# Memory keys and values of an encoder block: token-major product with k outermost and whole weight rows

## The chip, the cores and the metric

The kernel is one launch on one core of a Trainium2 chip. The metric is device time in microseconds (us), from the core's start to its end. The engines are named as the profile names them: PE (TensorE, matrix products), PEld (its loads of stationary operands), DVE (VectorE), ACT (ScalarE), POOL (GpSimd) and SP (SyncE, which here issues nearly all DMAs).

## The reference

One layer of a hybrid encoder block, 512 tokens by 1024 channels in fp32. Only the cross-attention branch to 256 memory tokens is shown in full, since the change lies there:

```python
h = rms_norm(x, norm_mix_pre[l])
z = h @ w_in[l]                    # qa, ka, va, qx, pin and the gates
oa = window_attention(qa, ka, va, rel_bias, sinks)   # 16 heads, 2 key groups, chunks of 64
mkv = rms_norm(mem, norm_mem[l]) @ w_mem_kv[l]       # (256, 1024) @ (1024, 1024)
mk, mv = jnp.split(mkv, 2, axis=-1)                  # keys and values, 4 heads of 128
ox = memory_attention(qx, mk, mv)
op = multiscale_pool(pin, w_pool_map[l], pool_scale[l])
merged = gates[0] * (oa @ w_branch_a) + gates[1] * (ox @ w_branch_x) + gates[2] * (op @ w_branch_p)
x = x + rms_norm(merged @ w_out[l], norm_mix_post[l])
# then a SwiGLU FFN with d_ff = 2816 between two RMS norms
```

## The kernel before, in words

Every fp32 product is made of three float32r products: an operand is split into a high part (`w_hi`, a rounding copy on ACT, line 403) and a low part (`w_lo`, the difference, on DVE, line 408), and hi·hi, hi·lo and lo·hi are summed in PSUM (`three`, line 1337). So every weight tile costs ACT and DVE a pass before PE can use it.

Work is laid out by `plan()` as 66 steps. A step is mostly one tile: 128 output channels over the whole contraction of 1024 (8 slices `k` of 128). Steps 0 to 7 are the memory projection (`mem` 4 to 7, the values, then `mem` 0 to 3, the keys), then `k`, `v`, eight `q`, four `qx`, four `pin`, gates and merges. Each engine has its own program, written by hand, which goes through the steps with a loop `for s in range(NS)`. In step s, ACT and DVE split the weights of step s + 2 into one of three slots `w_hi[s % 3]`, `w_lo[s % 3]`, which needs the product of step s - 1 to be over. Raw weights come in chunks of two steps (two loads of 512 KB) into `raw[0]`, `raw[1]` and, once, `raw_early`; SP issues all loads in the order of its program and waits on `weights_split` before it overwrites a buffer.

The memory projection is feature-major. A tile has weight columns as stationary operand and the 256 memory tokens as moving one: 24 products of 256 columns. ACT evicts the tile to `mvT` or `mk` (`take`, line 717). The first two tiles are made in two halves of the contraction (`first_tiles`), so that they can begin when half the tokens and half of a chunk have arrived. Before them PE runs 40 transposes of an identity matrix (`warm_up`, line 1472).

The norm of the memory tokens is applied after the product. Their sums of squares are made in step 9 (`mem_sum`), POOL raises them to the power -1/2, and then the scale takes two ways. For the keys, which have the tokens along the free axis, DVE builds two diagonal matrices (`mem_diagonal`, line 1075), PE spreads them over all partitions by a product with ones (`mem_scale`, line 1372, in step 11) and DVE multiplies `mk` (line 1058). For the values, PE transposes `mvT` after step 12 (line 1500) and DVE scales on the way out of PSUM (line 1153). In the same stretch the norm of x (loaded by SP only after the last split of the transposed x, on `turned_split`) becomes a row `x_row` (lines 1113, 1490, 1117), by which DVE scales `k`, `v` and `q` as it evicts them (lines 934 and 956).

The tiles of the first steps take PSUM banks 0 to 3 in turn; a tile waits until the tile before it in its bank is evicted. Attention units begin in step 15 (scores, bias, softmax, turn, output; one unit in two steps). In `maxima` DVE waits for the scores, for unit 0 first reverses the bias table (line 975), then adds the bias (line 978, two instructions), and for the first chunk pair overwrites the masked half with -1e30 (line 984).

## Time and profile before

| | |
|---|---|
| median of 3 runs | 802.42 us (802.08 to 802.8) |
| profiled execution, its own time | 802.09 us |
| its span in the trace | 800.3 us |
| PE busy | 788.7 us (99% of the span) |
| DVE busy | 481.0 us (60%) |
| ACT busy | 332.4 us (42%) |
| mean granted clock of TensorE | 0.998 |

The span is what the trace covers; the rest of the execution's time (1.79 us) lies around it. Products on PE are pipelined and their ends are modelled, so the distance between the starts of two products tells more than the length of one. Idle time of an engine costs something only where the engine is the one that is waited for.

### The profile page before, as it was taken

The numbers are of one execution on the slowest core, as the hardware profiler recorded it, in microseconds if no ns is written. First come the engines' busy times: TensorE is split into PE (matmuls) and PEld (weight loads), VectorE is DVE, ScalarE is ACT, GpSimd is POOL, SyncE is SP. The second block draws the span as 40 slices with busy tenths as digits, with TensorE's granted clock in tenths as the row PEclk, the third lists the DMA queues.
The fourth block names the chain that finished last, engine by engine and source line by source line (L and its number), as shares of the span: only waits on it lengthen the run. The fifth ranks groups of instructions, "written<-read, shape, count | busy, mean of one in ns | idle before, by whom it ended". The sixth has DMA issues, their size and how long they took to land.

```text
span 800.3 us, 11623 instructions
## 1 busy us (share of the span) xinstructions
PE 788.7 (99%) x4624; PEld 688.0 (86%) x4624; DVE 481.0 (60%) x597; ACT 332.4 (42%) x558; POOL 47.1 (6%) x99
## 2 busy tenths in 40 slices
PE   8999999999999999999999999999999999999997
PEld 7978778777778888888888999999999999888885
DVE  5755657666434633625655589888888887733222
ACT  5731544454335223223443455444444446632111
POOL 0020000444000000000001210000000000000000
PEclk9999999999999999999999999999999999999999
DMA  8961221312212333333371003333333344641011
GB/s 289 304 185 52 84 75 53 106 54 71 87 53 61 99 105 106 106 105 134 130 263 52 26 30 108 105 104 105 105 105 105 105 131 157 218 151 52 1 53 52
DMA packets 68502, 85.76 MB, mean 107 GB/s; under 512 B 3552, under 2 KB 61424, under 8 KB 68464
## 3 DMA queue, kind: packets, MB, share of 16 engines
q1 hardware_dynamic: 68288, 85.23, 32.5%
q8 instruction: 26, 0.43, 0.2%
q14 instruction: 12, 0.10, 0.0%
q10 hardware_dynamic: 176, 0.01, 0.0%
HBM read 83.12 MB, written 2.11 MB: 106 GB/s over the span
## 4 chain that ended last, share of the span: by engine, by line
PE 91%; DVE 4%; DMA 1%; issue 1%; ACT 1%; POOL 1%; SPq 0%; DVEq 0%; POOLq 0%; ACTq 0%
PE pair L1337 84%; PE pair L1446 1%; DMA raw<-in_w_mem_kv 1%; PE pair L1427 1%; PE pair L1460 1%; PE pair L1435 1%; PE pair L1465 1%; POOL B_f L657 1%; DVE T_f L1224 1%; DVE op_lo L1204 1%; DVE T_lo L1231 0%; PE pair L1361 0%; ACT probs L694 0%; DVE k_dup L934 0%; PE pair L1344 0%
## 5 line engine op out<-in xcount | busy, mean ns | idle before, releaser
L408 DVE TENSOR_TENSOR w_lo<-raw,w_hi 128x1024 fp32r<-128x1024 f32 x66 | 84.1, 1277 | 95.4 <-ACT w_hi L403 95.4
L1337 PE MATMUL pair<-hT_hi,w_hi 128*128 128x512 f32 x336 | 135.6, 403 | 0.0
L1337 PE MATMUL pair<-hT_hi,w_lo 128*128 128x512 f32 x336 | 131.2, 390 | 0.0
L1337 PE MATMUL pair<-hT_lo,w_hi 128*128 128x512 f32 x336 | 130.9, 390 | 0.0
L403 ACT ACTIVATE w_hi<-raw 128x1024 fp32r<-128x1024 f32 x66 | 69.5, 1055 | 105.8 <-PE pair L1337 90.1
L1337 PE MATMUL pair<-T_hi,op_hi 128*128 128x256 f32 x320 | 90.6, 283 | 0.5 <-DVE op_lo L1204 0.5
L1337 PE MATMUL pair<-T_lo,op_hi 128*128 128x256 f32 x320 | 90.6, 283 | 0.0
L1337 PE MATMUL pair<-T_hi,op_lo 128*128 128x256 f32 x320 | 90.5, 283 | 0.0
L1337 PEld LDWEIGHTS pair<-hT_hi,w_hi 128*128 128x128 f32 x336 | 63.1, 188 | 14.2 <-issue 1.0
L1337 PEld LDWEIGHTS pair<-hT_lo,w_hi 128*128 128x128 f32 x336 | 63.2, 188 | 13.4 <-issue 1.0
L1337 PEld LDWEIGHTS pair<-hT_hi,w_lo 128*128 128x128 f32 x336 | 63.0, 188 | 13.5
L1337 PE MATMUL pair<-wd_hi,df_hi 128*128 128x512 f32 x176 | 68.5, 389 | 0.0
L1337 PE MATMUL pair<-wd_lo,df_hi 128*128 128x512 f32 x176 | 68.5, 389 | 0.0
L1337 PE MATMUL pair<-wd_hi,df_lo 128*128 128x512 f32 x176 | 68.5, 389 | 0.0
L1337 PE MATMUL pair<-B_hi,op_hi 128*128 128x256 f32 x240 | 67.9, 283 | 0.0
L1337 PE MATMUL pair<-B_lo,op_hi 128*128 128x256 f32 x240 | 67.9, 283 | 0.0
L1337 PE MATMUL pair<-B_hi,op_lo 128*128 128x256 f32 x240 | 67.9, 283 | 0.0
L1337 PEld LDWEIGHTS pair<-T_hi,op_hi 128*128 128x128 f32 x320 | 61.4, 192 | 0.7 <-DVE op_lo L1204 0.7
L1337 PEld LDWEIGHTS pair<-T_hi,op_lo 128*128 128x128 f32 x320 | 61.4, 192 | 0.0
L1337 PEld LDWEIGHTS pair<-T_lo,op_hi 128*128 128x128 f32 x320 | 61.4, 192 | 0.0
L408 DVE TENSOR_TENSOR wd_lo<-raw,wd_hi 128x1024 fp32r<-128x1024 f32 x22 | 26.9, 1222 | 35.6 <-ACT wd_hi L403 35.6
L1337 PEld LDWEIGHTS pair<-B_hi,op_hi 128*128 128x128 f32 x240 | 46.1, 192 | 0.0
(194 smaller groups left out, 1549.5 us busy)
## 6 DMA issues: line engine op xcount, KB each, us to landing
raw<-in_w_in SPq DMA_DIRECT2D x42, 512.0 KB, 4.8
raw<-in_w_ffn_up SPq DMA_DIRECT2D x22, 512.0 KB, 4.7
raw<-in_w_ffn_gate SPq DMA_DIRECT2D x22, 512.0 KB, 4.2
raw<-in_w_ffn_down SPq DMA_DIRECT2D x22, 512.0 KB, 4.0
raw<-in_w_branch_a SPq DMA_DIRECT2D x8, 512.0 KB, 4.1
raw<-in_w_out SPq DMA_DIRECT2D x8, 512.0 KB, 3.6
raw<-in_w_mem_kv SPq DMA_DIRECT2D x6, 512.0 KB, 7.1
xT_in<-in_x_t SPq DMA_DIRECT2D x4, 512.0 KB, 8.8
```

What stands on the lines that cost most here:

```text
L403: eng.activation(split_at(s)[0], raw_view(s), ACT.Copy).then_inc(weights_hi, 1)
L408: eng.tensor_tensor(lo, raw_view(s), hi.bitcast(F32), ALU.subtract).then_inc(weights_split, 1)
L657: pool.tensor_tensor(plain[b][:, :, P * (t % 2):P * (t % 2) + P], h2_at(t, h, True).bitcast(F32), h2_at(t, h, False).bitcast(F32), ALU.add ...
L1204: dve.tensor_tensor(lo[:, :, :], op_source(m), hi[:, :, :].bitcast(F32), ALU.subtract).then_inc(ops_split, 1)
L1224: dve.tensor_tensor(plain[t][:, :, :], plain[a][:, :, :], plain[b][:, :, :], ALU.subtract)\
L1337: ins = pe.matmul(dst, a, b, start=first and n == 0, stop=last and n == 2, skip_group_check=onto)
L1427: ins = pe.matmul(scores[:, pr // 2, at:at + KEYS], q[lo:lo + 64, 2 * a + pr % 2, ch, :, :].rearrange("p j t -> p (j t)"), k_dup[lo:lo + 6 ...
L1435: ins = pe.matmul(scores[:, i // 2, at:at + N_MEM], qx[:, a, P * i:P * i + P], mk[:, a, :], start=True, stop=True)
L1446: ins = pe.transpose(turned[:, at // 4, P * (at % 4):P * (at % 4) + P], probs[:, i, :], ident[:, :])
L1460: ins = pe.matmul(bk(O_BANK)[64 * half:64 * half + 64, 2 * P * c:2 * P * c + 2 * P], v_c[:, 2 * b + c, 64 * a:64 * a + 64], probs[:, i:i + ...
L1465: ins = pe.matmul(bk(O_BANK), mv[:, m, a, :], probs[:, 4 * m:4 * m + 4, :], start=(m == 0), stop=(m == MT - 1))
```

## The change

The memory projection becomes token-major: the tokens are the stationary operand (128 tokens) and 512 weight columns the moving one. `k` is the outermost loop, and one step is one slice `k`: a whole weight row block of 128 x 1024 is loaded (4 KB in a row in memory, where before it was 1 KB), split, and multiplied into four PSUM banks that are open through all eight steps (banks 0 and 1 keys and values of tokens 0 to 127, banks 2 and 3 those of tokens 128 to 255). `k`, `v` and `mem_sum` get banks of their own (4, 5, 7). The transposed memory tokens come in four loads of 256 KB instead of two of 512 KB, and the first weight row in two halves of 256 KB; the loads of the transposed x move between them.

After the last row ACT evicts the four banks (`mem_take`), keys to `mk_rows` and values straight to `mv`. In step 10 DVE scales both by the token's norm, now one number per partition (4 instructions). After step 12 PE transposes `mk_rows` in place of `mvT`, and DVE copies the result to `mk`. `mem_diagonal` and `mem_scale` are gone.

DVE's instructions for `x_diag` move from step 10 to step 9, and the splits of x to steps 2, 4, 6 and 7. In `maxima`, the reversal of the bias and the masked half come ahead of the wait for the scores, and the first half of the masked units is added in two smaller instructions. POOL waits for the maxima of unit 4 before it begins the pooling branch.

```diff
-X_HI = {1: (0,), 3: (1,), 4: (2,), 5: (3,)}
-X_LO = {2: (0,), 4: (1,), 5: (2, 3)}
+X_SPLITS = {2: 0, 4: 1, 6: 2, 7: 3}
-    steps = [[("mem", h)] for h in (4, 5, 6, 7, 0, 1, 2, 3)]
+    steps = [[("mem", k)] for k in range(KT)]
-    steps[MEM_SUM + 2].append(("mem_scale", 0))
-        O_BANK, SUM_BANK = 3, 7
+        O_BANK, OUTER_BANK = 3, {"k": 4, "v": 5, "mem_sum": 7}
+        def mem_bank(m, h):
+            return bk(2 * m + h)
+            def load_row(k):
+                if k == 6:
+                    sp.wait_ge(weights_split, 4)
+                load_half(k // 2, k % 2, row_in[k])
+            load_mem(0)
+            load_half(0, 0, half_in, slice(0, 512))
+            load_half(0, 0, row_in[0], slice(512, 1024))
+            load_mem(1)
+            load_row(1)
+            load_row(2)
+            load_mem(2)
+            load_row(3)
+            load_mem(3)
+            load_row(4)
             load_x(0)
+            load_row(5)
+            load_row(6)
             load_x(1)
+            load_row(7)
+            load_chunk(4)
             load_x(2)
             load_x(3)
+            def mem_take(m, h):
+                act.wait_ge(tile_full, KT)
+                dst = mv[:, m, :, :] if h else as4(mk_rows[:, m, :])
+                act.activation(dst, as4(mem_bank(m, h)), ACT.Copy).then_inc(mem_rows_out, 1)
             def mem_evicted(t):
                ...
+                dve.wait_ge(mem_rows_out, 2 * MT)
+                for m in range(MT):
+                    dve.wait_ge(mem_rstd_ready, m + 1)
+                    for rows in (as4(mk_rows[:, m, :]), mv[:, m, :, :]):
+                        dve.tensor_scalar(rows, rows, rstd[:, c + m:c + m + 1], None, ALU.mult).then_inc(mem_scaled, 1)
-                if s == X_SCALE:
+                if s == X_SQUARES:
                     for t in range(TT):
                         dve.wait_ge(rstd_ready, NORM_X + t + 1)
             def maxima(u):
                 kind, a, b = unit_of(u)
+                if u == 0:
+                    dve.wait_ge(bias_loaded, 16 * 16)
+                    ...
+                    link(dve.tensor_copy(bias[:, :, :, :].rearrange("p g a k -> p (g a) k"), back))
+                    dve.wait_ge(smalls_loaded, 16 * 4)
+                if kind == "a" and b == 0:
+                    if u >= 1:
+                        dve.wait_ge(o_full, u)
+                    dve.memset(probs[:, 0:4, 0:CHUNK], -1e30).then_inc(masked, 1)
                 dve.wait_ge(scores_full, u + 1)
-            first_tiles()
-            for s in range(2, NS):
+            for k in range(KT):
+                mem_row(k)
+            for s in range(KT, NS):
+            def mem_row(k):
+                def part(m, h):
+                    cols = slice(4 * h, 4 * h + 4)
+                    whi, wlo = (w[k % 3][:, cols, :].rearrange("p a c -> p (a c)") for w in (w_hi, w_lo))
+                    return three(mem_bank(m, h), whi, wlo, memT_hi[:, k, P * m:P * m + P], memT_lo[:, k, P * m:P * m + P],
+                                 k == 0, k == KT - 1, swap=True)
+                pe.wait_ge(mem_split, k + 1)
+                ...
+                    pe.wait_ge(weights_split, k + 1)
+                    for m in range(MT):
+                        for h in range(2):
+                            ins = part(m, h)
```

Two places show how the instructions move. The first is PE at the start of the projection. In these rows `w_hi_51`, `w_hi_52` and `w_hi_53` are the three weight slots, `w_lo_55` the low part of the first, and `pair` is PSUM. Before:

```order
L1472 MATMUL pair<-ident 128x128 x39
L1337 MATMUL pair<-memT_hi,w_hi_51 128x256 [waits mem_split,half_split,ones_ready]
L1337 MATMUL pair<-memT_lo,w_hi_51 128x256
L1337 MATMUL pair<-memT_hi,w_lo_55 128x256
L1337 MATMUL pair<-memT_hi,w_hi_51 128x256 [waits mem_split]
...
L1337 MATMUL pair<-memT_hi,w_hi_52 128x256 [waits half_split]
...
L1337 MATMUL pair<-memT_hi,w_hi_51 128x256 [waits mem_split,weights_split]
```

After:

```order
L1517 MATMUL pair<-ident 128x128 x39
L1379 MATMUL pair<-w_hi_51,memT_hi 128x512 [waits half_split,mem_split,ones_ready]
L1379 MATMUL pair<-w_lo_55,memT_hi 128x512
L1379 MATMUL pair<-w_hi_51,memT_lo 128x512
L1379 MATMUL pair<-w_hi_51,memT_hi 128x512
...
L1379 MATMUL pair<-w_hi_51,memT_hi 128x512 [waits weights_split]
...
L1379 MATMUL pair<-w_hi_52,memT_hi 128x512 [waits weights_split,mem_split]
...
L1379 MATMUL pair<-w_hi_53,memT_hi 128x512 [waits weights_split,mem_split]
```

The products of the first row need one load of tokens and one half row. A row's twelve products are 512 columns wide, and from the second row on each row has one wait for its weights and its tokens.

The second place is DVE from the diagonals of x to the eviction of the projected `v`, steps 9 to 11. Before:

```order
L1113 TENSOR_SCALAR x_diag<-ident,rstd 128x128 [waits rstd_ready] x4
L1054 TENSOR_SCALAR meansq<-pair 128x2 [waits tile_full]
L408 TENSOR_TENSOR w_lo_56<-raw_49,w_hi_52 128x1024 [waits weights_hi]
L1117 COPY x_row<-pair 128x512 [waits x_scaled]
L934 TENSOR_TENSOR k_dup<-pair,x_row 64x512 [waits tile_copied,pads_ready,tile_full,x_row_ready]
L934 TENSOR_TENSOR k_dup<-pair,x_row 64x512 x3
L956 TENSOR_TENSOR vT<-pair,x_row 128x512 [waits tile_full]
L956 TENSOR_TENSOR q<-pair,x_row 128x8x64 [waits tile_full]
L1075 TENSOR_SCALAR diag<-ident,rstd 128x128 [waits mem_rstd_ready] x2
L408 TENSOR_TENSOR w_lo_57<-raw_50,w_hi_53 128x1024 [waits weights_hi]
L956 TENSOR_TENSOR q<-pair,x_row 128x8x64 [waits tile_full]
L1058 TENSOR_TENSOR mk<-mk,pair 128x1024 [waits tile_copied,tile_full]
```

After:

```order
L1158 TENSOR_SCALAR x_diag<-ident,rstd 128x128 [waits rstd_ready] x4
L415 TENSOR_TENSOR w_lo_55<-raw_49,w_hi_51 128x1024 [waits weights_hi]
L1100 TENSOR_SCALAR meansq<-pair 128x2 [waits tile_full]
L1105 TENSOR_SCALAR mk_rows<-mk_rows,rstd 128x512 [waits mem_rstd_ready,mem_rows_out]
L1105 TENSOR_SCALAR mv<-mv,rstd 128x512
L1105 TENSOR_SCALAR mk_rows<-mk_rows,rstd 128x512 [waits mem_rstd_ready]
L1105 TENSOR_SCALAR mv<-mv,rstd 128x512
L415 TENSOR_TENSOR w_lo_56<-raw_49,w_hi_52 128x1024 [waits weights_hi]
L1162 COPY x_row<-pair 128x512 [waits x_scaled]
L969 TENSOR_TENSOR k_dup<-pair,x_row 64x512 [waits pads_ready,tile_full,x_row_ready]
L969 TENSOR_TENSOR k_dup<-pair,x_row 64x512 x3
L991 TENSOR_TENSOR vT<-pair,x_row 128x512 [waits tile_full]
```

The diagonals of x stand ahead of a weight split that they followed. The four scalings of keys and values stand ahead of the split of step 13 and of the evictions of `k` and `v`; the diagonals of the memory norm and the scaling of `mk` are gone.

## Rows read from the trace of the kernel before

**Rows 1.** page, part 1, and waits of the whole run (engine line waited for: us, times, longest)
```profile
PE 788.7 (99%) x4624; PEld 688.0 (86%) x4624; DVE 481.0 (60%) x597; ACT 332.4 (42%) x558; POOL 47.1 (6%) x99
...
PE pair L1372 <- DVE diag L1075: 1.3, 1, 1.3
...
PE pair L1337 <- DVE w_lo L408: 0.5, 1, 0.5
PE pair L1337 <- DVE op_lo L1204: 0.5, 1, 0.5
```

**Rows 2.** windows (stretch, busy per engine, PEclk, DMA share, GB/s)
```profile
2.00:29.00 27.00, 25.20 (x198) 24.79 (x199) 17.48 (x53) 18.75 (x33) 0.24 (x2) 1.00 0.96 311
```

**Rows 3.** timeline of PE (start, duration, line, operation [idle before <- releaser])
```profile
2.05 6.04 PE L1472 MATMUL pair<-ident 128*128 128x128 f32 x40 [2.05 <-POOL ident L597]
9.33 0.36 PE L1337 MATMUL pair<-memT_hi,w_hi 128*128 128x256 f32 x1 [1.24 <-issue]
...
15.04 0.28 PE L1337 MATMUL pair<-memT_hi,w_lo 128*128 128x256 f32 x1
15.82 0.38 PE L1337 MATMUL pair<-memT_hi,w_hi 128*128 128x256 f32 x1 [0.51 <-DVE w_lo L408]
...
33.19 0.40 PE L1337 MATMUL pair<-hT_hi,w_hi 128*128 128x512 f32 x1
```

**Rows 4.** timelines of ACT and DVE, the first 23 us
```profile
6.28 1.71 ACT L737 ACTIVATE memT_hi<-memT_in,g_mem_c 128x256 fp32r<-128x256 f32 x4 [3.13 <-DMA memT_in<-in_mem]
7.89 1.13 ACT L742 ACTIVATE w_hi<-raw 128x512 fp32r<-128x512 f32 x2
...
19.02 1.06 ACT L403 ACTIVATE w_hi<-raw_early 128x1024 fp32r<-128x1024 f32 x1 [2.06 <-DMA raw_early<-in_w_mem_kv]
...
6.90 1.67 DVE L1082 SCALAR_TENSOR_TENSOR memT_lo<-memT_in,g_mem_c,memT_hi 128x256 fp32r<-128x256 f32 x4 [6.90 <-ACT memT_hi L737]
8.54 1.29 DVE L1089 TENSOR_TENSOR w_lo<-raw,w_hi 128x512 fp32r<-128x512 f32 x2
...
16.82 2.04 DVE L1144 COPY rel_row<-relT 16x18 f32<-16x18 f32 x29
...
20.11 1.23 DVE L408 TENSOR_TENSOR w_lo<-raw_early,w_hi 128x1024 fp32r<-128x1024 f32 x1 [1.24 <-ACT w_hi L403]
21.25 1.41 DVE L919 SCALAR_TENSOR_TENSOR hT_lo<-xT_in,g_pre_c,hT_hi 128x512 fp32r<-128x512 f32 x2
```

**Rows 5.** DMA issues up to 34 us (KB each, median us to landing)
```profile
xT_in<-in_x_t SPq DMA_DIRECT2D x4, 512.0 KB, 8.8
```

**Rows 6.** chain of waits, one tile (start, us, what)
```profile
44.60 5.62 PE pair L1337 x24
```

**Rows 7.** timeline of PE, around that wait and unit 0's turn
```profile
56.16 0.39 PE L1337 MATMUL pair<-hT_hi,w_lo 128*128 128x512 f32 x1
57.84 0.68 PE L1372 MATMUL pair<-diag,ones 128*128 128x128 f32 x4 [1.29 <-DVE diag L1075]
58.28 0.48 PE L1337 MATMUL pair<-hT_hi,w_hi 128*128 128x512 f32 x1
...
86.44 0.39 PE L1337 MATMUL pair<-hT_hi,w_lo 128*128 128x512 f32 x1
87.04 1.09 PE L1446 MATMUL pair<-ident,probs 128*128 128x128 f32 x8 [0.21 <-DVE probs L1006]
```

**Rows 8.** timelines of DVE and ACT, 31 to 92 us
```profile
66.87 1.40 DVE L1153 TENSOR_SCALAR mv<-pair,rstd 128x512 f32<-128x512 f32 x2
...
77.81 0.69 DVE L975 COPY bias<-bias_back 128x1024 f32<-128x1024 f32 x1 [3.56 <-PE pair L1427]
...
39.82 1.04 ACT L676 ACTIVATE square<-x_in 128x1024 f32<-128x1024 f32 x1
...
91.27 0.60 ACT L707 ACTIVATE oa_hi<-pair 128x512 fp32r<-128x512 f32 x1 [2.06 <-PE pair L1460]
```

**Rows 9.** chain of waits, output projection
```profile
423.65 10.93 PE pair L1337 x48
```

More of the change, by code:

```diff
@@ L129, in encoder_block @@
     UNIT0 = steps.index([("q", 5)])
-    copied_kinds = ("mem", "k", "v", "q", "qx", "pin", "gate")
+    copied_kinds = ("k", "v", "q", "qx", "pin", "gate")
     copied_no, merged_no = {}, {}
     for t in tiles:
-        d = copied_no if t[0] in copied_kinds else merged_no
-        d[t] = len(d) + 1
+        if t[0] != "mem":
+            d = copied_no if t[0] in copied_kinds else merged_no
+            d[t] = len(d) + 1
     def ap(t, offset, pattern):
@@ L275, in encoder_block @@
             last = {b: m for m, b in enumerate(bank_of)}
-            b = SUM_BANK if t[0] == "mem_sum" else min(range(free), key=lambda i: last.get(i, -1))
+            b = OUTER_BANK[t[0]] if t[0] in OUTER_BANK else min(range(free), key=lambda i: last.get(i, -1))
             bank_of.append(b)
             bank_before[n] = last.get(b)
-        last_in_o_bank = max(n for n, b in enumerate(bank_of) if b == O_BANK and n < step_end[UNIT0])
         first_in_o_bank = min(n for n, b in enumerate(bank_of) if b == O_BANK and n >= step_end[UNIT0])
+        def mem_bank(m, h):
+            return bk(2 * m + h)
         def sem(name):
@@ L285, in encoder_block @@
         raw_in = [sem(f"raw_in{i}") for i in range(2)]
-        early_in = sem("early_in")
-        mem_loaded = [sem(f"mem_loaded{i}") for i in range(2)]
+        mem_rows_out, mem_scaled = sem("mem_rows_out"), sem("mem_scaled")
+        mem_loaded = [sem(f"mem_loaded{i}") for i in range(MEM_PIECES)]
+        row_in = [sem(f"row_in{k}") for k in range(KT)]
         x_loaded = [sem(f"x_loaded{i}") for i in range(TT)]
@@ L338, in chunk_halves @@
                 if t == "mem":
-                    v, col = w_mem_v, P * i
-                elif t == "a":
+                    return [w_mem_kv[P * (i + h):P * (i + h + 1), :] for h in range(2)]
+                if t == "a":
                     v, col = wa_v, P * i
@@ L519, in _ @@
             sp.dma_start(scale_p[:, :], pool_scale).then_inc(smalls_loaded, 16)
-            for c in range(4, 6):
-                load_chunk(c)
+            load_chunk(5)
             sp.wait_ge(turned_split, KT)
@@ L634, in _ @@
                 pool.wait_ge(tile_copied, copied_no[("pin", g)])
+                if g == 0:
+                    pool.wait_ge(neg_max_ready, (steps.index([("pin", 0)]) - UNIT0) // 2 + 2)
                 if g >= 1:
@@ L1126, in _ @@
                     for t in steps[s - 1]:
-                        if t in copied_no and t[0] not in ("mem", "k", "v"):
+                        if t in copied_no and t[0] not in ("k", "v"):
                             scaled_take(t)
@@ L1368, in tile @@
                     return
-                if kind == "mem_scale":
-                    pe.wait_ge(diag_ready, MT)
-                    for m in range(MT):
-                        ins = pe.matmul(dst[:, P * m:P * m + P], ones[:, :], diag[:, m, :], start=True, stop=True)
-                    ins.then_inc(tile_full, 1)
-                    return
                 whi, wlo = w_hi[s % 3], w_lo[s % 3]
                 pe.wait_ge(weights_split, at_stream[("step", s)] + 1)
-                if kind == "mem":
-                    xhi, xlo, dst = memT_hi, memT_lo, dst[:, 0:N_MEM]
-                elif kind in ("a", "p", "x"):
+                if kind in ("a", "p", "x"):
                     xhi, xlo = {"a": (oa_hi, oa_lo), "p": (op_hi, op_lo), "x": (ox_hi, ox_lo)}[kind]
@@ L1454, in unit_out @@
                 else:
-                    pe.wait_ge(tile_copied, copied_no[tiles[last_in_o_bank]])
+                    pe.wait_ge(mem_rows_out, O_BANK + 1)
                 if kind == "a":
```

163 lines of the change are left out of this document (83 added, 80 removed).

## The prediction

> **What bounds the kernel now.** I read first the busy times and the list of what PE waited for [rows 1]. PE is busy for 99% of the span, and of its named waits inside the program only one is over a microsecond: 1.3 us for DVE's diagonals of the memory norm. The others are 0.5 us in the memory projection and 0.5 us in the FFN. So this is a PE-bound program: what counts is the distance between starts of products, the few holes between them, and when the first real product can begin. The granted clock is 1.00 in the projection [rows 2], which is the upper level, 2.4 GHz. Next I read PE's timeline at the start [rows 3]: warm-up transposes from 2.05 to 8.09, a hole, the first product at 9.33, a second hole before 15.82, and the first product of `k` at 33.19. Then the timelines of ACT and DVE, which make the operands [rows 4], and the loads [rows 5]. Last come the pace of a 512-column product in this stretch [rows 6], the two later places where PE waits [rows 7], the costs of copies and scalings [rows 8], and the pace of the output projection [rows 9], whose products have the form that the changed projection will have (weights moving, tokens stationary).
>
> Since almost nothing after unit 0 waits for an absolute time, a microsecond won before 90 us should arrive at the end as a microsecond. The loads there follow the splits, so they move with PE.
>
> **Start of the first product.** Before, ACT begins at 6.28, when the 512 KB of tokens have come, makes four token slices (1.71) and the halves of two tiles (1.13 for two), and DVE's first low part begins at 8.54 and takes 0.65 (half of 1.29) [rows 4]; PE follows at 9.33 [rows 3]. After, PE needs two token slices (0.86) and one half row (0.57), then DVE's 0.65: 2.1 us and some 0.15 of handing over, so 2.25 after the tokens land. They land at 6.28 at the latest, as the 512 KB did, and 256 KB must be earlier; halving only the transfer at 311 GB/s [rows 2] takes 0.8 us off, so 5.5. PE could begin at 7.75, but the warm-up ends at 8.09 and is now what is late. I take 8.1: **1.2 us won**. Bounds: 0.8 (tokens at 6.28, so PE at 8.5) and 1.25.
>
> **The hole inside the projection.** 15.04 to 15.82 is 0.78 where a product takes 0.12, so 0.66 is lost to waiting for the low part of the third tile [rows 3]. That wait is one for a chunk of two tiles. After, the equivalent is row 1. It lies behind 1.5 MB of loads, as the second half of the tokens did before; that half was there when ACT wanted it at 9.0 (7.89 plus 1.13, and no wait), so row 1 lands by 9.0, and at the mean rate of 311 GB/s from 2 us on by 7.1 [rows 2]. Add 1.06 on ACT and 1.23 on DVE [rows 4]: ready between 9.5 and 11.4. PE asks for it after twelve products, at 8.1 + 12 x 0.234 = 10.9. So a stall of 0 to 0.5; I take 0.2. Net **0.66 - 0.2 = 0.46 won**.
>
> **The products.** Before: 33.19 - 9.33 = 23.86, less 0.66, is 23.2 us for 192 products of 256 columns, 0.121 each. After: 96 of 512 columns. In the row just behind the projection 24 such products take 5.62 us, 0.234 each [rows 6]; in the output projection 48 take 10.93, 0.228 each [rows 9]. The nearer row was taken under full DMA load like the projection, so I use it: 96 x 0.234 = 22.5, and 0.1 for the first. **0.6 us won**; by the other row 1.3, which is the far bound. On the near side I set 0.4.
>
> **The norm's diagonal.** In step 11 the last product of `q` 1 starts at 56.16 and the first of `q` 2 at 58.28 [rows 7]: 2.12 where 0.23 is usual. The wait of 1.29 for DVE's diagonals and the products with ones both go. **1.89 won**, if DVE isn't late for something else. What is late next there are the transposes after step 12, which wait for the evicted `v` and now for the scaled keys. I follow DVE: x is loaded for its squares only after the last split of x, which stays near 31 us, so ACT can begin the squares as before at 39.82 [rows 8] at the latest; four of them, 1.04 each and a read-out, some 1.2 together, end at 44.6; POOL and the four diagonals, now ahead of a split, bring DVE to 45.7. Behind that wait stands the split of step 12, which PE wants at 54, so the earlier place costs nothing. Then split 1.23, the mean square, POOL's two powers (1.1), four scalings at the 0.70 that a 128 x 512 scaling out of PSUM takes [rows 8], split of step 13, `x_row` 0.7, four `k_dup` at 0.7 and `v` 0.7: 45.7 + 1.2 + 1.3 + 2.8 + 1.2 + 0.7 + 2.8 + 0.7 = 56.4. PE gets to the transposes at 8.1 + 0.2 + 22.6 = 30.9 for the end of the projection, then five tiles of 5.62 and 0.7 of small products: 59.7. The cover is 3.3 us, so the added 2.8 us of scaling cost nothing. The four evictions on ACT are 0.60 each [rows 8] and end by 34.5; `q` 0 wants its bank at 42.5. If the cover were gone, each microsecond of DVE would be one of PE.
>
> **Splits during the projection.** PE takes 2.8 us a row, ACT 1.06 and DVE 1.23, plus tokens and x (DVE 0.42 a token slice, 0.70 a slice of x, [rows 4]). The tightest point is row 4: from 11.4 on DVE has the splits of rows 2 and 3 (2.5), four token slices (1.7) and the `rel_row` copies (2.04 [rows 4]), 17.6, and the split ends at 18.9; PE wants it at 8.3 + 4 x 2.81 = 19.5. Covered by 0.6. The last slices of x end near 31.4; `k` wants them at 35.8.
>
> **Unit 0.** The turn of its probabilities waits 0.21 [rows 7]. DVE's reversal of the bias, 0.69 [rows 8], leaves the chain ahead of it, so the wait goes: **0.2 won**. For unit 4 the masked half was not on PE's path; the POOL wait stands behind maxima that DVE does before it evicts `pin` 0, so it releases nothing later. Both at nothing, and a few tenths either way at most.
>
> **Sum.** 1.2 + 0.46 + 0.6 + 1.89 + 0.2 = 4.35. The profiled execution took 802.09, so 797.7. The median of the runs is 802.42, 0.33 above it, so on that scale 798.1; I say 798.0. The bounds together: won at least 0.8 + 0.16 + 0.4 + 1.6 + 0 = 3.0 and at most 1.25 + 0.66 + 1.3 + 1.9 + 0.4 = 5.5, so 796.7 to 799.4.
>
> **Rivals.** *Late rows.* PE no longer works on two tiles from half a chunk but waits for each row; if the loads come slower than before, the holes come back eight times. Row 4 must have landed by 17.1 (19.5 less the two splits): that is 1 MB of tokens and 2.6 MB of weights in 15 us, 245 GB/s, against a mean of 311 in this stretch [rows 2]. At 200 GB/s it would land at 20.4 and PE would stand for 3.3 us: 801.3 us. For it: smaller first loads, and the trace has no row-wise load in this stretch. Against it: the rate, and rows four times as long in memory. The Trainium skill's page "DMA: Bandwidth & Descriptors", section "Measured (HBM→SBUF, 128 partitions, SWDGE, issued from GpSimd)", asks for batches of 1 MiB or more for 75% of peak, which speaks against pieces of 256 KB; here loads of 512 KB already run at 311 GB/s together, because several are in flight, so I give it little. The page "TensorE: Matmul & The Clock Gate", section "HAM oscillation — how this bites in real kernels", has a loop over k whose waits for loads make the array fall back to the slow clock; the trace's own holes of 1.24 and 0.51 us [rows 3] left the granted clock at 1.00 [rows 2], so it belongs to this rival only. *DVE takes the place of the removed wait.* The queue of step 10 and 11 grows past its 3.3 us of cover and PE stands before the transposes for what it won at the diagonal: 798.1 + 1.9 = 800.0. Against it is the working above; for it, that POOL's powers and ACT's evictions are waited for in a row. *Slower than before.* One mechanism: the last slices of x. SP holds row 6 back until row 3 is split, and row 7, the weights of `k` and `v` and the last two loads of x queue behind it. `k` wants the last slice at 35.8; its load must be in by 33.4. Up to it there are 8.4 MB, which came by 29 us before (311 GB/s from 2 us on). To end over 804.0 PE must lose 6 us here, so the load must end at 39.4, a mean of 225 GB/s; that is where it decides, and it would give 804 to 806. Loads of x did take 8.8 us to land in the median [rows 5], but queued, not slow. *Faster still*: products at 0.228 and no stall at row 1, 0.9 more: 797.2 or a little less.
>
> **Chances.** Forecast, with its own range of 796.9 to 799.2: 0.76. Faster still, 796.2 to 796.9: 0.06. Late rows, 799.2 to 801.5: 0.09. DVE, near 800: 0.05. Slower: 0.04. Range for 8 in 10: 796.7 to 800.2. What a measurement of this kernel can tell from no change is 0.2%, 1.6 us, so faster means under 800.8: 0.76 + 0.06 + 0.05 + half of the late rows is 0.91; within 0.05; slower 0.04.
>
> **What would show it.** The first product of the projection near 8.1, directly behind the warm-up; a hole under 0.5 us before row 1 and none before other rows; 96 products 0.228 to 0.234 apart; `k` beginning near 30.9 instead of 33.19; no wait between `q` 1 and `q` 2, none at the transposes, none at unit 0's turn; from there on every stretch as long as before. A first product later than 8.6, a granted clock under 1.00, or a wait of PE for DVE at the transposes would make it wrong.

## The result, and the profile after

The changed kernel takes 798.53 us in the median, the kernel before 802.42. The ratio is 0.9949, with a 95% interval of 0.9937 to 0.9962: 0.5% faster, clear of no change. One of the changed kernel's five executions took 2791 us, a slow run that isn't in the ratio; the other four took 798.0 to 798.5. The profiled execution took 798.53 us with a span of 796.7; before they were 802.09 and 800.3, so the two traces differ by 3.6 us, and this is what has to be found.

The page, part 1, and what PE waited for, as in [rows 1]:

```profile
PE 787.0 (99%) x4524; PEld 683.4 (86%) x4524; DVE 481.4 (60%) x599; ACT 332.6 (42%) x553; POOL 47.7 (6%) x99
...
PE pair L1379 <- DVE w_lo L415: 1.3, 1, 1.3
```

PE is as full as before. The wait for the diagonals (1.3) and the one in the projection (0.5) are gone, and a new one of 1.3 stands in the projection, for DVE's low part of a weight row. Next PE's timeline from the start to the first product of `k`; the columns are those of [rows 3]:

```profile
2.05 6.82 PE L1517 MATMUL pair<-ident 128*128 128x128 f32 x40 [2.05 <-POOL ident L620]
8.63 0.47 PE L1379 MATMUL pair<-w_hi,memT_hi 128*128 128x512 f32 x1
...
11.25 0.39 PE L1379 MATMUL pair<-w_hi,memT_lo 128*128 128x512 f32 x1
12.97 0.47 PE L1379 MATMUL pair<-w_hi,memT_hi 128*128 128x512 f32 x1 [1.33 <-DVE w_lo L415]
...
32.13 0.39 PE L1379 MATMUL pair<-hT_hi,w_hi 128*128 128x512 f32 x1
```

The first product begins at 8.63 instead of 9.33. The twelfth begins at 11.25, and the next one, row 1's first, would be due at 11.48 and begins at 12.97: 1.49 us lost, where the kernel before lost 0.66 [rows 3]. `k` begins at 32.13 instead of 33.19. There is no idle time before rows 2 to 7. The timelines of ACT and DVE say what row 1 waited for, and answer to [rows 4]:

```profile
5.59 0.91 ACT L758 ACTIVATE memT_hi<-memT_in,g_mem_c 128x256 fp32r<-128x256 f32 x2 [2.45 <-DMA memT_in<-in_mem]
...
9.24 0.91 ACT L758 ACTIVATE memT_hi<-memT_in,g_mem_c 128x256 fp32r<-128x256 f32 x2 [1.10 <-DMA memT_in<-in_mem]
10.51 1.06 ACT L410 ACTIVATE w_hi<-raw 128x1024 fp32r<-128x1024 f32 x1 [0.36 <-DMA raw<-in_w_mem_kv]
...
7.07 0.69 DVE L1131 TENSOR_TENSOR w_lo<-raw,w_hi 128x512 fp32r<-128x512 f32 x1
...
11.60 2.52 DVE L415 TENSOR_TENSOR w_lo<-raw,w_hi 128x1024 fp32r<-128x1024 f32 x2 [0.93 <-ACT w_hi L410]
```

ACT stands until row 1's load has landed at 10.50, splits it until 11.57, DVE makes its low part from 11.60 to 12.83, and PE starts at 12.97. Ahead of that, ACT had waited 1.10 us for the second piece of tokens, which landed at 9.24, and which only row 2 needs. The rates are in the windows of the same stretch, the kernel after first, the one before second (columns as in [rows 2]):

```profile
2.00:9.00 7.00, 6.95 (x42) 6.91 (x43) 2.23 (x4) 3.21 (x6) 0.24 (x2) 1.00 0.88 247
2.00:10.50 8.50, 8.45 (x48) 8.14 (x49) 2.95 (x6) 4.12 (x8) 0.24 (x2) 1.00 0.90 276
9.00:15.00 6.00, 4.67 (x21) 3.53 (x20) 4.22 (x7) 5.07 (x8) 0.00 (x0) 1.00 1.03 415
```

```profile
2.00:9.00 7.00, 6.04 (x40) 5.80 (x40) 2.10 (x5) 3.86 (x9) 0.24 (x2) 1.00 0.95 296
9.00:15.00 6.00, 5.67 (x47) 5.70 (x48) 4.07 (x9) 4.30 (x9) 0.00 (x0) 1.00 1.08 361
```

Up to 9 us the kernel after moved 1.73 MB (7 us at 247 GB/s), the kernel before 2.07 MB. From 9 to 15 it is the other way round: 415 GB/s where weights come in rows of 4 KB, 361 where they come in pieces of 1 KB. Order and mix of the loads differ too, so these numbers alone don't show that the row length does it. When row 1 had landed, 2.35 MB had moved (8.5 us at 276 GB/s), though in order of issue row 1 ends after 1.57 MB.

The chain of waits shows the rest. First after, then the rows of before that were not needed ahead of the prediction; columns are start, length, what:

```profile
43.18 0.34 PE pair L1410 x4
...
50.02 10.90 PE pair L1379 x48
60.92 0.88 PE pair L1547 x8
...
73.56 1.09 PE pair L1473 x16
...
83.73 0.87 PE pair L1491 x8
...
86.68 1.01 PE pair L1505 x8
...
403.97 15.27 PE pair L1379 x66
```

```profile
44.26 0.34 PE pair L1366 x4
...
64.00 0.87 PE pair L1500 x8
...
76.67 1.12 PE pair L1427 x16
...
90.20 1.01 PE pair L1460 x8
...
407.51 15.26 PE pair L1337 x66
```

Read as a ledger (before minus after; what each stretch added is the difference of two lines):

| event | before | after | won so far |
|---|---|---|---|
| first product | 9.33 | 8.63 | 0.70 |
| first product of `k` | 33.19 | 32.13 | 1.06 |
| `mem_sum`, after `k` and `v` | 44.26 | 43.18 | 1.08 |
| transposes after step 12 | 64.00 | 60.92 | 3.08 |
| scores of unit 0 | 76.67 | 73.56 | 3.11 |
| turn of unit 0 | 87.04 | 83.73 | 3.31 |
| output of unit 0 | 90.20 | 86.68 | 3.52 |
| output projection | 407.51 | 403.97 | 3.54 |
| span | 800.3 | 796.7 | 3.6 |

Everything is won before 90 us and kept for the other 710. The two `q` tiles between which PE used to stand for the diagonals are now one piece of 10.90. DVE's queue there, which the prediction added up, answers to [rows 8]:

```profile
47.54 1.23 DVE L415 TENSOR_TENSOR w_lo<-raw,w_hi 128x1024 fp32r<-128x1024 f32 x1 [2.45 <-ACT w_hi L410]
...
49.57 0.49 DVE L1105 TENSOR_SCALAR mk_rows<-mk_rows,rstd 128x512 f32<-128x512 f32 x1 [0.73 <-POOL rstd L648]
...
50.77 0.48 DVE L1105 TENSOR_SCALAR mv<-mv,rstd 128x512 f32<-128x512 f32 x1
...
55.84 0.69 DVE L991 TENSOR_TENSOR vT<-pair,x_row 128x512 f32<-128x512 f32 x1
```

The four scalings take 0.40 each from start to start, and `v` is evicted at 56.53, while PE wants it at 60.92: a cover of 4.4 us.

### The profile page after: what moved, and what is told of

Its sections match the earlier page's. It is cut to its first block, busy times and chain, and to the rows that moved or that the text cites. A ratio compares the mean times of both kernels' runs of the same rounds, so it can differ in the third digit from the quotient of the medians.

```text
span 796.7 us, 11430 instructions
## 1 busy us (share of the span) xinstructions
PE 787.0 (99%) x4524; PEld 683.4 (86%) x4524; DVE 481.4 (60%) x599; ACT 332.6 (42%) x553; POOL 47.7 (6%) x99
## 4 chain that ended last, share of the span: by engine, by line
PE 93%; DVE 3%; DMA 1%; issue 1%; POOL 1%; ACT 1%; SPq 0%; DVEq 0%; POOLq 0%; ACTq 0%
PE pair L1379 87%; PE pair L1491 1%; PE pair L1473 1%; PE pair L1505 1%; DMA raw<-in_w_mem_kv 1%; PE pair L1480 1%; PE pair L1510 1%; POOL B_f L682 1%; DVE T_f L1266 1%; DVE op_lo L1246 1%; DVE T_lo L1273 0%; PE pair L1405 0%; PE pair L1386 0%; DVE sum_odd L1261 0%; DVE f L1278 0%
```

## The experiments

Each kernel was timed beside the kernel before, in three groups: experiments 1 to 4, 5 to 8 and 9 to 11. "Ratio" is to the kernel before in the same group, with its 95% interval. The kernel before took 802.31, 802.24 and 802.00 us in them, so medians of different groups can differ by 0.3 us without any change. One thousandth is 0.8 us. The later stretch repeats closely: from `mem_sum` to the output projection, a stretch that only experiment 5 changes, the two traces of the changed kernel and those of its other eight variants below agree within 0.05 us (360.78 to 360.83).

**1. The diagonal alone.** In the kernel before, `mem_diagonal` goes ahead of `x_row` and the evictions of `k`, `v` and `q`, and nothing else changes:

```diff
                 if s == X_SCALE + 1:
+                    mem_diagonal()
                     dve.wait_ge(x_scaled, 1)
-                if s == MEM_SUM + 2:
-                    mem_diagonal()
```

> The kernel before, with DVE's two diagonals of the memory norm moved ahead of the copy of x_row and the evictions of k, v and q 0 in step 11. The products with ones stay. If the 1.97 us between q 1 and q 2 were a wait of 1.3 for DVE's queue plus 0.7 of products, the wait goes and the span falls by 1.3 us (802.1 to 800.8), PE going straight from q 1 to the products with ones. Rival: the wait is set by the norm itself (POOL's powers, at 49 us) or by the eviction of k, whose bank q 2 or the scale takes; then PE still waits there, less than 0.4 us is won.

Measured: 801.27 us, ratio 0.9987 (0.9978 to 0.9997). Its chain of waits:

```profile
56.46 0.59 PE pair L1371 x4
...
57.06 5.74 PE pair L1336 x24
```

The diagonal product no longer waits. The first product of `q` 2 begins 0.99 us behind the last of `q` 1, where it was 2.12 [rows 7] and is 0.23 in the changed kernel. So 1.13 of the 1.89 us there, six tenths, could be had by moving one call: the wait was one of order on DVE, not of a late result from POOL. The rest, 0.76, is the products with ones, which the token-major form makes needless. The output projection begins at 406.27 instead of 407.51, 1.24 earlier, of which 0.09 was there before `mem_sum` and has nothing to do with this edit.

**2. Is the warm-up what holds the start?** The record of the warm-up ends at 8.87, past the start of the first product, and the operands were ready at 7.76 (DVE's first low part, 7.07 plus 0.69, above). So, 32 transposes instead of 40:

```diff
-WARM_UP = 40
+WARM_UP = 32
```

> The changed kernel with 32 transposes of warm-up in place of 40. Theory: row 1's weights gate the projection, so the first product comes some 0.6 to 0.9 us earlier (8.63 to about 7.8) and the hole before row 1 grows by as much (1.33 to about 2.1); row 1 stays near 13.0 and the time stays at 798.5 within 0.2. Rival: the first product's start gates it (as the prediction counted it), then 0.6 to 0.8 us less: 797.8. A second rival: fewer transposes leave the array at its lower clock when the products begin, then the first row runs at half pace and the time is the same or up to 1 us more.

Measured: 798.46 us, ratio 0.9949 (0.9932 to 0.9965), the same as the changed kernel. PE's timeline:

```profile
8.26 0.47 PE L1379 MATMUL pair<-w_hi,memT_hi 128*128 128x512 f32 x1 [1.16 <-DVE w_lo L1131]
...
12.85 0.47 PE L1379 MATMUL pair<-w_hi,memT_hi 128*128 128x512 f32 x1 [1.61 <-DVE w_lo L415]
```

The warm-up ended at 7.11. The first product came 0.37 earlier, but waited for its own operands by then, and row 1 began at 12.85 against 12.97: the hole took all of the gain. Row 1's arrival sets the end of this stretch, and no earlier start helps.

**3. Row 1 ahead of the second piece of tokens.** Only the order of issue changes, on SP, ACT and DVE. PE wants that piece only for row 2:

```diff
-            load_mem(1)
             load_row(1)
+            load_mem(1)
             load_row(2)
...
-            mem_hi(1)
             split_hi(act, 1)
+            mem_hi(1)
...
-            mem_lo(1)
             split_lo(dve, 1)
+            mem_lo(1)
```

> The changed kernel with the load of weight row 1 ahead of the second load of tokens, and its split on ACT and DVE ahead of that token piece too (rows 0 and 1 need only the first piece). If row 1 is late because 256 KB of tokens it doesn't need stand ahead of it on the queue and on both engines: 0.26 MB less ahead at some 390 GB/s is 0.65 us, so row 1's load lands near 9.8, products of row 1 begin near 12.2, and the time falls by 0.7 us to 797.8. Rival: the loads in flight share the engines, so that order hardly matters; then row 1 lands within 0.2 us of 10.5 and nothing changes.

Measured: 797.40 us, ratio 0.9938 (0.9921 to 0.9954). ACT's timeline at row 1, then the chain of waits:

```profile
9.22 1.06 ACT L410 ACTIVATE w_hi<-raw 128x1024 fp32r<-128x1024 f32 x1 [0.65 <-DMA raw<-in_w_mem_kv]
```

```profile
2.05 7.11 PE pair L1517 x40
9.16 32.70 PE pair L1379 x144
```

Row 1 is split from 9.22, 1.3 us earlier than before, and the hole is gone: 144 products stand in one piece. The output projection begins at 402.65, 1.32 before the changed kernel's and 1.00 before that of its second profile (experiment 11); in the medians of this group it is 1.06 (experiment 2 took 798.46). That is more than the 0.7 expected. ACT's and DVE's order moved together with the load, but in the changed kernel ACT was done with the tokens at 10.15 and stood until the load landed at 10.50, so there it was the load that was late. The cover is thin: row 1's low part was done at 11.54, and PE took it up at 11.76. The first product began only at 8.92, behind a warm-up of 7.11.

**4. `k` and `v` in the banks of rows.** The changed kernel with `k` and `v` in banks 0 and 1:

```diff
-        O_BANK, OUTER_BANK = 3, {"k": 4, "v": 5, "mem_sum": 7}
+        O_BANK, OUTER_BANK = 3, {"k": 0, "v": 1, "mem_sum": 7}
...
-                    pe.wait_ge(mem_rows_out, O_BANK + 1)
+                    pe.wait_ge(tile_copied, copied_no[("q", 3)])
```

> The changed kernel with k and v in banks 0 and 1, which the projection uses, in place of banks 4 and 5. All four banks of the projection become free only after its last row, and ACT evicts the first at 34.6 us, behind the squares of the tokens. Theory: k can't begin at 32.1 but at 34.7, PE stands for 2.5 us with nothing to fill it: 801.0 us. Rival: the evictions hide because k's first products wait only a short while, or ACT gets to them earlier since it waits for nothing: under 1 us more.

Measured: 802.30 us, ratio 0.9994 (0.9984 to 1.0004), 1.3 above the 801.0 expected: in the median all that the change wins is lost. PE's timeline and three windows:

```profile
31.82 0.39 PE L1379 MATMUL pair<-w_hi,memT_lo 128*128 128x512 f32 x1
34.24 0.50 PE L1379 MATMUL pair<-hT_hi,w_hi 128*128 128x512 f32 x1 [2.03 <-ACT mk_rows L764]
...
36.25 0.63 PE L1379 MATMUL pair<-hT_lo,w_hi 128*128 128x512 f32 x1
36.68 0.63 PE L1379 MATMUL pair<-hT_hi,w_lo 128*128 128x512 f32 x1
```

```profile
34.00:36.00 2.00, 1.75 (x7) 1.43 (x8) 0.00 (x0) 2.00 (x5) 0.00 (x0) 0.91 0.86 293
36.00:38.00 2.00, 2.00 (x7) 1.54 (x6) 1.38 (x2) 0.59 (x1) 0.00 (x0) 0.50 1.00 354
38.00:40.00 2.00, 2.00 (x8) 1.64 (x7) 1.93 (x3) 0.00 (x0) 0.00 (x0) 0.74 1.00 392
```

The last row's product starts at 31.82, and `k` 2.42 later instead of 0.23, because ACT evicts the banks behind work of its own. Then comes a cost that nothing in the sum held: the granted clock falls to 0.50, the lower level of 1.2 GHz, and products stand 0.43 apart. The 48 products of `k` and `v` take 12.82 us where the changed kernel takes 11.05 (32.13 to 43.18). So 2.2 us of waiting and 1.8 us of clock, against 3.9 lost at the output projection (407.86 and 403.97). The ten executions scatter as if the fall didn't always come: seven took 802.1 to 802.8, three only 800.5 to 801.3, near the 800.7 that the wait alone would make of 798.5. Only one was profiled, one of the seven, so this isn't shown. The banks of their own are a necessary part of this change, though no term of the sum named them. The Trainium skill, page "TensorE: Matmul & The Clock Gate", section "HAM oscillation — how this bites in real kernels", describes a loop whose waits for loads throw the array back to the slow clock. This trace agrees in kind: the clock fell after 2.03 us of idle PE, while 1.66 us before row 1 in the same execution left the products 0.23 apart.

**5. The old order in `maxima`.** The changed kernel with `maxima` as before: bias copy and masked half behind the wait for the scores.

```diff
-                if u == 0:
-                    ...                      # bias copy
-                if kind == "a" and b == 0:
-                    ...                      # masked half
                 dve.wait_ge(scores_full, u + 1)
+                    if u == 0:
+                        ...                  # bias copy
...
-                        dve.wait_ge(masked, a + 1)
+                        link(dve.memset(probs[:, 0:4, 0:CHUNK], -1e30))
```

> The changed kernel with maxima as before (reversal of the bias and masked half behind the wait for the scores, two full additions). Theory: the chain of unit 0 grows by 0.7 + 0.3 + 0.1 us and the turn of its probabilities waits again, about 0.2 us of idle time and 0.2 of a slower first product, so span and time 0.4 us more (798.9). Units 1 to 7 unchanged; unit 4 hidden. Rival: it is not unit 0 but the projection's shift that took the wait away; then nothing changes.

Measured: 798.63 us, ratio 0.9956 (0.9939 to 0.9972). The wait is back:

```profile
83.09 1.09 PE L1479 MATMUL pair<-ident,probs 128*128 128x128 f32 x8 [0.21 <-DVE probs L1041]
```

The time itself tells nothing, since its row 1 came at 12.14 by chance. The stretch from `mem_sum` to the output projection, which row 1 doesn't touch, tells: 42.34 to 403.55 is 361.21 us, in the changed kernel 43.18 to 403.97 is 360.79. So the new order is worth 0.42 us: 0.2 of waiting, and 0.2 for the eight transposes behind the wait, which take 1.09 against 0.87.

**6. Are later loads what delays row 1?** SP holds row 2 and everything behind it until the first half row has landed:

```diff
             load_row(1)
+            sp.wait_ge(half_in, 16)
             load_row(2)
```

> The changed kernel with SP holding the load of row 2 and all behind it until the first half of row 0 has landed (about 6.4 us; before, row 2 was issued at 3.6). Theory of shared engines: row 1's load landed at 10.5 although 1.58 MB ended with it and 2.3 MB had moved, so later loads took 0.7 MB of its time; held back, row 1 lands 1 us or more earlier (9.3) and its products begin near 11.8, time 797.5. Rival: loads complete in the order of issue and the slow first 5 us (66 to 300 GB/s) are what delays row 1; then it lands within 0.3 us of 10.5 and later rows come later without being waited for: 798.5.

Measured: 799.21 us, ratio 0.9965 (0.995 to 0.9979). PE's timeline at rows 1 and 4:

```profile
11.98 0.47 PE L1380 MATMUL pair<-w_hi,memT_hi 128*128 128x512 f32 x1 [0.58 <-DVE w_lo L415]
...
21.67 0.47 PE L1380 MATMUL pair<-w_hi,memT_hi 128*128 128x512 f32 x1 [0.89 <-DVE w_lo L415]
```

ACT had row 1 at 9.52, 1.0 earlier than in the changed kernel. But experiment 5, which holds nothing back, had it at 9.68, so this doesn't show that sharing is what delays it. It does show that few bytes before 9 us aren't enough as a reason: here they were as few as in the changed kernel (247 GB/s from 2 to 9 us in both), and row 1 was there a microsecond earlier. What differed is how much had moved in all by then: 1.94 MB here (258 GB/s to 9.52), 2.05 in experiment 5 (267 to 9.68), 2.35 in the changed kernel. Of these, 1.57 MB were needed, so the later row 1 landed, the more bytes of loads behind it had moved before it. What sets that share stays open. The price of holding loads back shows as well: row 4 came late, PE stood for 0.9 us, and the output projection began at 404.51.

**7. Row 1 in halves too.** Experiment 3 with row 1 loaded and split in two halves, like row 0:

```diff
+                if k == 1:
+                    load_half(0, 1, row_in[1], slice(0, 512))
+                    load_half(0, 1, row1_b, slice(512, 1024))
+                    return
...
-                if k == 0:
-                    pe.wait_ge(half_split, 1)
+                if k <= 1:
+                    pe.wait_ge((half_split, row1_split)[k], 1)
```

> Row 1's load ahead of the second token piece as in the run before, and row 1 also in two halves of 256 KB with their own splits, so that PE can begin on half a row. Since with row 1 first the hole was gone, theory says that the projection now depends on the first product's start (end of the warm-up, 8.9 to 9.2) alone: nothing more is won, 797.4 within 0.2. Rival: row 1's readiness still sets the pace through the split engines, then up to 0.5 us less.

Measured: 797.13 us, ratio 0.9937 (0.992 to 0.9953). With the hole closed there is little left here. But against the expectation it was not the end of the warm-up that set the first product:

```profile
8.73 0.47 PE L1392 MATMUL pair<-w_hi,memT_hi 128*128 128x512 f32 x1 [0.61 <-DVE w_lo L1139]
```

The warm-up ended at 8.13, and the product waited for its own operands.

**8. All together.** Experiment 7, with the gain vector of the tokens loaded from ACT's queue instead of SP's, so that the tokens are issued first, and 30 transposes:

```diff
-WARM_UP = 40
+WARM_UP = 30
...
-            sp.dma_start(g_mem_c[:, :], g_mem).then_inc(gain_loaded["mem"], 16)
             load_mem(0)
...
+            act.dma_start(g_mem_c[:, :], g_mem).then_inc(gain_loaded["mem"], 16)
             act.dma_start(g_pre_c[:, :], g_mix_pre).then_inc(gain_loaded["pre"], 16)
```

> As the run with row 1 in halves, and the 4 KB gain load that stands first on SP's queue moved to ACT's queue (the token load issues 0.45 us earlier), and 30 transposes of warm-up in place of 40. Theory: with row 1 out of the way the first product's start is what counts; its operands are ready 0.45 us earlier than with the gain in front (near 8.1) and the warm-up ends by 7, so the first product comes at 8.1 instead of 8.9 and the time falls by 0.8 us to 796.6. Rival: the array is still or again at its lower clock at that moment, and the first row at half pace costs back what the start won: 797.4 or more, with a granted clock under 1.00 in the first 12 us.

Measured: 796.13 us, ratio 0.9924 (0.9908 to 0.9941), the fastest version. PE's timeline and chain:

```profile
7.75 0.47 PE L1392 MATMUL pair<-w_hi,memT_hi 128*128 128x512 f32 x1 [0.90 <-DVE w_lo L1139]
```

```profile
7.75 32.97 PE pair L1392 x144
```

The start moves to 7.75, no hole opens, and the output projection begins at 401.50, 2.47 before the changed kernel's. An earlier start, worth nothing in experiment 2, is worth 1.0 us (797.13 to 796.13, with the first product at 8.73 and 7.75) once row 1 no longer gates. The two edits weren't tried apart. In experiment 7 the product waited for operands and not for the warm-up, so the earlier loads are needed; 40 transposes ended at 8.0 at the earliest (experiment 4), so 7.75 needs the shorter warm-up too. ACT could begin on the tokens at 5.16 to 5.45 in the three profiles with the gain on its own queue (here and in experiments 9 and 10), and then waited for that gain; with the gain on SP's queue it was 5.46 to 6.43, for the tokens.

**9. 256 columns.** Experiment 8 with each product of 512 columns made as two of 256:

```diff
-                    return three(mem_bank(m, h), whi, wlo, ...)
+                    for i in range(2):
+                        c = slice(2 * P * i, 2 * P * i + 2 * P)
+                        ins = three(mem_bank(m, h)[:, c], whi[:, c], wlo[:, c], ...)
+                    return ins
```

> The fastest kernel so far (row 1 first and in halves, gain on ACT's queue, 30 transposes of warm-up) with the projection's products 256 columns wide in place of 512, so 192 in place of 96, layout and loads unchanged. Theory: the step named the products is a matter of width: 192 at 0.121 (23.2 us) against 96 at 0.229 (22.0), so the projection takes 1.2 us more and the time 1.2 us more (797.3). Rival: in the kernel before the 0.121 came from the operands' kind or the crowded loads, not from the width; then nothing changes.

Measured: 797.32 us, ratio 0.994 (0.9924 to 0.9957). From the first product to `k` it takes 23.09 us, against 21.92 in experiment 8: 192 products 0.120 apart against 96 at 0.228: 1.17 us. The time is 1.19 more, across two groups. That is the term "products", by itself: a matter of width.

**10. Four transposes.** Experiment 8 with `WARM_UP = 4`:

> The same kernel with 4 transposes of warm-up in place of 30. Its first product comes at 7.75 whatever the warm-up does. Theory: the array then begins the projection at its lower clock: products 0.43 apart as in the run with shared banks, until the clock rises, some 9 to 16 of them, so 1.8 to 3.2 us more (798 to 799.3) and a granted clock under 1.00 in the stretch from 7.7 to 12. Rival: the row loads hide it (row 2 isn't ready much before PE wants it), then under 1 us more.

Measured: 798.07 us, ratio 0.9951 (0.9934 to 0.9967). PE's timeline and the window of its slow products:

```profile
7.62 0.77 PE L1392 MATMUL pair<-w_hi,memT_hi 128*128 128x512 f32 x1 [4.45 <-DVE w_lo L1139]
...
11.17 0.63 PE L1392 MATMUL pair<-w_hi,memT_lo 128*128 128x512 f32 x1
11.60 0.49 PE L1392 MATMUL pair<-w_hi,memT_hi 128*128 128x512 f32 x1
11.92 0.40 PE L1392 MATMUL pair<-w_lo,memT_hi 128*128 128x512 f32 x1
```

```profile
7.60:11.60 4.00, 3.98 (x10) 3.17 (x11) 2.69 (x6) 3.08 (x6) 0.00 (x0) 1.00 1.00 394
```

The first nine products stand 0.43 apart (0.56 behind the very first), as at 0.50 in experiment 4, and from 11.60 on they stand 0.23 to 0.32 apart. To `k` it takes 23.83 us against 21.92: 1.9 us, and the time is 1.94 more, again across two groups. The other 26 transposes are worth that. The column of the granted clock says 1.00 here all the same, so at the program's start the spacing has to be read, not the column. (The prediction read the column for the kernel before [rows 2]; there the 0.121 between products bears it out.) The Trainium skill, page "TensorE: Matmul & The Clock Gate", section "Wait — 56ns, not 53.3ns?", gives 426.7 ns between products of 512 columns at 1.2 GHz, and the trace agrees with 0.43; for 2.4 GHz it gives 215.7 ns, where this kernel's products stand 0.227 to 0.229 apart, and the measurement decides.

**11. The changed kernel again**, unchanged, in the group of 9 and 10.

> The changed kernel as it is, profiled once more beside the two others. Row 1's load landed at 10.4 to 10.5 in three profiles of this order of loads and at 9.7 in two (one of them with the later loads held back). Theory: this scatter of up to 0.8 us belongs to the loads of the first microseconds and not to the edits; products of row 1 begin between 12.1 and 13.0, first product between 8.2 and 8.7, time 798.5 within 0.3.

Measured: 798.14 us, ratio 0.9949 (0.9933 to 0.9966), the first ratio once more, and just under the time expected, in a group where the kernel before was 0.3 to 0.4 us faster as well. The first product began at 8.36, row 1's at 12.68: a hole of 1.48 again. ACT had row 1 at 10.21, when 2.35 MB had moved (286 GB/s from 2 us on), as in the first profile. The warm-up's 40 transposes took 6.45 here, 6.82 in the first profile, 6.04 before the change [rows 3].

## Why the prediction came near, step by step

The mechanism was right in the large: a PE-bound program, wins before 90 us arriving at the end undiminished. The forecast of 798.0 (797.7 on the profile's scale) is 0.5 to 0.8 below what was measured. That it is so near is in part luck. Start and hole together were to win 1.66 and lost 0.13, an error of 1.79; the other terms brought 0.98 more than forecast and hid over half of it. Two of the prediction's own signs of being wrong came true: the first product later than 8.6, if only by 0.03, and a hole of 1.49 where it wanted less than 0.5, so that `k` began at 32.13 and not near 30.9. (Its bounds, 3.0 to 5.5 won, give 796.9 to 799.4 on the scale of the medians; the 796.7 mixes the two scales.)

| term | predicted | measured | shown by |
|---|---|---|---|
| first product | +1.2 | +0.70 | the timelines |
| hole in the projection | +0.46 | -0.83 | the timelines; 2 and 3 |
| products | +0.6 | +1.19 | the timelines; 9 |
| norm's diagonal | +1.89 | +2.00 | the chain; 1 |
| unit 0 | +0.2 | +0.41 | the chain; 5 |
| the rest | 0 | +0.07 | |
| sum | 4.35 | 3.54 | |

*The hole* is the step that failed, and it has the wrong sign. The prediction said that row 1 "lands by 9.0", since before the second half of the tokens, behind as many bytes, was there when ACT wanted it. It landed at 10.50. I had seen only that the old load was no later than 9.0 and took a rate, 311 GB/s, that is a mean over 27 us. Two things in the traces go with the 1.5 us. Until 9 us less was moved, 1.73 MB against 2.07; by experiment 6 that can't be all of it. And by 10.5 us 2.35 MB had moved, enough for all up to row 1 and one and a half loads behind it: a load that is in flight beside others doesn't finish when the bytes up to its place in the queue have moved. The Trainium skill, page "DMA: Bandwidth & Descriptors", section "Queues, rings and completion order", says that loads of one queue start in order but needn't complete in it. This trace bears out half of that: up to row 1 the loads landed in the order of issue, but later ones had moved bytes by then, 2.35 against 1.57 MB. Experiments 2 and 3 show what follows: an earlier start gave nothing, an earlier row 1 gave 1.0 to 1.3 us. The rival *late rows* had this mechanism but named the wrong row: it computed a hole at row 4, where loads had caught up at 415 GB/s, and not at row 1, where the rate of the first microseconds counts.

*The start.* The tokens did come early: ACT began at 5.59, where 5.5 was predicted, and the operands were ready at 7.76, where 7.75 was. That agreement is luck too: in experiments 2, 4 and 5, with the same loads up to there, ACT began at 5.64 to 5.98 and the first product waited for its operands until 8.26, 8.29 and 8.53. The warm-up, which I took at 6.04 for granted, took 6.82. Over the nine profiles with the same 40 transposes it took 5.96 (experiment 4) to 7.38 (experiment 1, whose edit lies far behind it), so this is a scatter of executions and not a cost of the change. The page "TensorE: Matmul & The Clock Gate" of the Trainium skill, section "What's actually happening", says that the moment at which the fast clock comes varies between runs of one kernel. The traces agree: the transposes go from 5 to 7 in a microsecond to 12 in the window from 5 to 6 us in experiment 4, from 7 to 8 in the changed kernel and from 8 to 9 in experiment 1. Since row 1 gated the stretch anyway, it cost the end nothing: experiment 2.

*The products.* 23.50 us less the hole of 1.49 is 22.01 for 96, 0.229 each. I chose 0.234 [rows 6] over 0.228 [rows 9], and misread it. The 24 products of [rows 6] hold one slow start behind products of another form:

```profile
44.46 0.49 PE L1337 MATMUL pair<-hT_hi,w_hi 128*128 128x512 f32 x1
44.78 0.40 PE L1337 MATMUL pair<-hT_lo,w_hi 128*128 128x512 f32 x1
```

That is 0.32 for the first. From the second product to the first one behind the tile, at 50.05, it is 0.229 for each of 23, the price that was measured. Dividing all by 24 spread the one slow start over the rest, and the prediction then added 0.1 for it once more. So the near row and the far one agree, whichever operand moves. Experiment 9 gives the price of the width without anything else: 1.17 us.

*The diagonal and the scalings* went as worked out, 2.00 for 1.89. The extra tenth is of the same sort as in the products: behind a wait or behind products of another form, the first product is followed after 0.31 us instead of 0.23 (12.97 and 13.28 in the changed kernel, 58.28 and 58.59 at the diagonal before). The cover was 4.4 us instead of 3.3, but not because DVE was early: it was done with `v` at 56.53, where 56.4 was predicted, by two errors that cancel. The split of step 12 began at 47.54 and not at 45.7, since ACT's high part came late, and from there to the end it took 9.0 us and not 10.7, mainly since a scaling between SBUF tiles costs 0.40 and not the 0.70 of one out of PSUM. What grew the cover is PE, which came to the transposes at 60.92 and not at 59.7, held up by row 1. *Unit 0* won twice what the idle time said, since the transposes behind the wait had been slower as well (experiment 5). *Splits* never gated behind row 1, *DVE in place of the wait* and *slower by the last slices of x* did not come: `k` started without a wait.

The moved splits and diagonals of x and POOL's wait were not tried alone; all that no term of the table explains comes to 0.07 us.

What stays open: why row 1's first product scatters over 0.8 us (12.14 to 12.97 in five profiles that load it in the same order), why fewer bytes move before 9 us than in the kernel before, and what share of them goes to loads that aren't needed yet. Experiment 6 was meant to tell sharing from a slow start and could not.

## What to carry to other kernels

When a fine-grained pipeline replaces a coarse one, ask for each of the first pieces when it *lands*, from the rate of the first microseconds and with the loads behind it counted as competitors, not from a mean rate; and issue in the order in which the array will want things. Shortening what is ahead of a gate is worth nothing until the gate moves: a shorter warm-up gave nothing while row 1 was late, and with row 1 issued first it gave, together with an earlier gain vector, 1.0 us. Take the price of a product from the distances between starts inside a row, and what its first product costs more apart from that: a mean over a whole tile mixes the two.

## What the runs showed of the hardware

- The clock fell after one short stall: 2.0 us of idle PE in the middle of a busy stretch (experiment 4), then some 3 us with products 0.43 apart. That wait cost nearly twice its length (2.2 and 1.8 us).
- At the program's start the record of the granted clock reads 1.00 while products stand 0.43 apart (experiment 10).
- With loads of 512 KB in 4 KB rows, several in flight, 415 GB/s moved from 9 to 15 us; in the kernel before, with pieces of 1 KB, 361. From 2 to 9 us it was 247 and 296 in these two traces. The same load of row 1 was taken up by ACT at 9.68 (experiment 5) to 10.51.
- 512-column products of this kernel stand 0.227 to 0.229 us apart, 256-column ones 0.120, and the first behind a wait or another form costs some 0.08 more.
- The same 40 transposes at the program's start took 5.96 to 7.38 us in nine profiles.
